# Second projection of 16 expert tiles: fp32 matmuls against three fp32r products of high and low halves

## The reference

```python
def hier_moe(u, wg, bg, we, be, w_gate, w_up, w_down):
    ...  # top-1 group, top-2 experts in it, weights in `combine`
    h = jax.nn.silu(jnp.einsum('bld,edf->blef', u, w_gate)) * jnp.einsum('bld,edf->blef', u, w_up)
    return jnp.einsum('blef,ble,efd->bld', h, combine, w_down)
```

## Time and profile before

| | |
|---|---|
| median of 3 runs | 643.33 us (642.3 to 643.43) |
| the profiled execution | 642.99 us |
| its span, first to last instruction | 641.1 us |
| PE busy | 606.9 us, 95% |
| DVE busy | 441.7 us, 69% |
| ACT busy | 304.5 us, 47% |
| POOL busy | 197.2 us, 31% |
| mean granted TensorE clock | 0.989 |

### The profile page before, as it was taken

The page is one execution under the profiler, slowest core; times in us unless marked ns, Lnnn a source line. Parts: engine busy times, 40 slices in busy tenths (PEclk is TensorE's granted clock), DMA queues, the critical chain, the costliest instruction groups (busy, mean ns, idle before and its releaser), DMA issues.

```text
span 641.1 us, 9310 instructions
## 1 busy us (share of the span) xinstructions
PE 606.9 (95%) x3342; PEld 455.6 (71%) x3342; DVE 441.7 (69%) x754; ACT 304.5 (47%) x503; POOL 197.2 (31%) x159
## 2 busy tenths in 40 slices
PE   6899999999999989998999999989999999999794
PEld 2237899999999966567888888656676776765241
DVE  4957776834993664466662698979998887761197
ACT  2749122334435534006895333926656665753144
POOL 1002333345561307141593071321211212211431
PEclk9999999999999999999999999999999999999798
DMA  8886856574721279855870824968999999999687
GB/s 302 356 274 252 281 183 188 184 236 150 231 80 65 91 255 335 320 210 165 274 238 8 291 73 164 321 243 335 357 389 412 393 384 395 374 352 388 219 263 131
DMA packets 47872, 162.88 MB, mean 254 GB/s; under 512 B 7073, under 2 KB 24865, under 8 KB 35282
## 3 DMA queue, kind: packets, MB, share of 16 engines
q1 hardware_dynamic: 34392, 118.03, 52.0%
q0 software_dynamic: 7712, 20.65, 10.4%
q10 hardware_dynamic: 5722, 23.60, 9.6%
HBM read 140.79 MB, written 31.36 MB: 269 GB/s over the span
## 4 chain that ended last, share of the span: by engine, by line
PE 82%; DVE 7%; DMA 6%; ACT 2%; issue 2%; ACTq 0%; DVEq 0%; POOLq 0%; POOL 0%
PE bank L1886 14%; PE bank L1566 12%; PE bank L1567 12%; PE bank L1940 9%; PE bank L1762 9%; DMA arena<-in_w_mod 3%; PE bank L1402 3%; PE bank L1873 3%; PE bank L1739 3%; PE bank L1666 2%; PE bank L1469 2%; PE bank L2005 2%; PE bank L1722 2%; PE bank L1997 1%; PE bank L1617 1%
## 5 line engine op out<-in xcount | busy, mean ns | idle before, releaser
L746 POOL TENSOR_TENSOR w_low<-arena,w_high 128x1024 fp32r<-128x1024 f32 x22 | 54.1, 2463 | 147.5 <-ACT w_high L954 147.5
L2533 DVE TENSOR_TENSOR gate_up_low<-arena,gate_up_high 128x1024 fp32r<-128x1024 f32 x64 | 75.3, 1221 | 13.1 <-ACT gate_up_high L1238 11.4
L1238 ACT ACTIVATE gate_up_high<-arena 128x1024 fp32r<-128x1024 f32 x64 | 63.9, 1054 | 15.4 <-DMA arena<-in_moe_w_gu 15.4
L954 ACT ACTIVATE w_high<-arena 128x1024 fp32r<-128x1024 f32 x22 | 23.2, 1059 | 87.4 <-PE bank L1567 85.4
L1566 PE MATMUL bank<-u_high,w_high 128*128 128x320 f32 x176 | 56.3, 320 | 1.7 <-DVE u_low L2146 1.7
L1940 PE MATMUL bank<-arena 128*128 128x512 f32 x128 | 57.7, 593 | 0.0
L1567 PE MATMUL bank<-u_high,w_low 128*128 128x320 f32 x176 | 54.4, 309 | 0.0
L1566 PE MATMUL bank<-u_low,w_high 128*128 128x320 f32 x176 | 54.4, 309 | 0.0
L1566 PE MATMUL bank<-u_high,w_low 128*128 128x320 f32 x176 | 54.4, 309 | 0.0
L1567 PE MATMUL bank<-u_low,w_high 128*128 128x320 f32 x176 | 54.4, 309 | 0.0
L1567 PE MATMUL bank<-u_high,w_high 128*128 128x320 f32 x176 | 54.4, 309 | 0.0
(11 more groups left out here) (440 smaller groups left out, 1405.8 us busy)
## 6 DMA issues: line engine op xcount, KB each, us to landing
arena<-in_moe_w_gu SPq DMA_DIRECT2D x38, 1024.0 KB, 11.9
arena<-in_w_mod SPq DMA_DIRECT2D x24, 1024.0 KB, 7.1
y_scr<-arena SPq DMA_DIRECT2D x26, 512.0 KB, 8.5
arena<-in_moe_w_down ACTq DMA_DIRECT2D x13, 1024.0 KB, 9.8
arena<-in_w_in SPq DMA_DIRECT2D x11, 1024.0 KB, 6.5
arena<-in_moe_w_down SPq DMA_DIRECT2D x6, 1024.0 KB, 10.4
arena<-in_x SPq DMA_DIRECT2D x10, 512.0 KB, 7.7
arena<-in_rpb SPq DMA_DIRECT2D x32, 128.0 KB, 3.2
```

Of the source, the lines that this page charges most:

```text
L746: G.tensor_tensor(WL[s_][:, :, w], ring[s_][:, :, w], WH[m % 2].bitcast(F), ALU.subtract).then_inc(wl_rdy, 1)
L954: S.activation(WH[m % 2], ring[(m // 2) % 2][:, :, (m % 2) * P:(m % 2 + 1) * P], ACT.Copy).then_inc(wh_rdy, 1)
L1238: S.activation(WGH[j][c], raw_gu[s][:, c, :, :], ACT.Copy).then_inc(wgh_rdy, 1)
L2533: tt_(WGL[s][c], raw_gu[s][:, c, :, :], WGH[j][c].bitcast(F), ALU.subtract).then_inc(wgl_rdy, 1)
```

## The change

The second projection of the static tiles is made of three fp32r products. ScalarE writes the high half of the transposed hidden rows (`hidden_high`) and, in a buffer of its own for each of the two row blocks k, the high half of the down weights (`down_high`, two instructions behind `hidden_high`). VectorE writes the low half of the hidden rows (`hidden_low`, behind the routing work, in front of pieces 2 and 3), and now increments `ht_ev`. GpSimd writes the low half of the down weights in place (`down_low`, two instructions, called in iteration n for tile n-2, behind the gather of n and the scatter of n-4). TensorE's `down` issues 12 matmuls in place of 4. In GpSimd's queue the scatter of tile 15 goes behind the overflow gather. The overflow step's own second projection stays fp32.

```diff
+        WDL = [split_view(f"down_low{s}", RAW_DN[s], 2, D) for s in range(3)]
+        WDH_AT = [MTAT + 4096, AFTER1 + 12288]
+        WDH = [split_view(f"down_high{k}", WDH_AT[k], 1, D)[:, 0, :] for k in range(2)]
+        HTH = [split_view(f"hidden_high{j}", HTAT + 512 * j, 2, P) for j in range(2)]
+        HTL = [split_view(f"hidden_low{j}", HTAT + 512 * j + 256, 2, P) for j in range(2)]
...
# GpSimd
+            def down_low(n):
+                for k in range(2):
+                    eng.wait_ge(wh_rdy, 30 + 2 * n + k + 1)
+                    G.tensor_tensor(WDL[n % 3][:, k, :], raw_dn[n % 3][:, k, :], WDH[k].bitcast(F), ALU.subtract).then_inc(wl_rdy, 1)
...
                 if n >= 4:
                     rows_scattered(n - 4)
-            for n in range(NE - 3, NE):
-                rows_scattered(n)
+                if n >= 2:
+                    down_low(n - 2)
+            rows_scattered(NE - 3)
+            down_low(NE - 1)
+            rows_scattered(NE - 2)
             eng.wait_ge(slots_rdy, 3)
...
                 token_rows(1, tokens_ov[:, :])
+            rows_scattered(NE - 1)
...
# ScalarE
-            def hidden_copy(n, j):
-                since(eng, ht_mm, n + 1)
-                since(eng, dn_mm, n - 1)
-                S.activation(hT[j][:, :, :], B[6][:, 0:2 * P].rearrange("p (a b) -> p a b", a=2), ACT.Copy
-                             ).then_inc(ht_ev, 1)
+            def hidden_high(n, j):
+                eng.wait_ge(ht_mm, n + 1)
+                since(eng, dn_mm, n - 1)
+                S.activation(HTH[j], B[6][:, 0:2 * P].rearrange("p (a b) -> p a b", a=2), ACT.Copy).then_inc(uth_rdy, 1)
+            def down_high(n):
+                eng.wait_ge(wdn_in[n % 3], 16 * (n // 3 + 1))
+                since(eng, dn_mm, n)
+                for k in range(2):
+                    S.activation(WDH[k], raw_dn[n % 3][:, k, :], ACT.Copy).then_inc(wh_rdy, 1)
...
-                hidden_copy(n, j)
+                hidden_high(n, j)
+                down_high(n)
...
# TensorE, down(n, j, s)
-                since(eng, ht_ev, n + 1)
-                since(eng, wdn_in[s], 16 * (n // 3 + 1))
+                eng.wait_ge(ht_ev, n + 1)
                 since(eng, y_evA, n)
                 since(eng, y_evB, n)
-                for b in range(2):
-                    for k in range(2):
-                        last = mm(B[4 + b][:, :], hT[j][:, k, :], raw_dn[s][:, k, b * 512:(b + 1) * 512],
-                                  start=(k == 0), stop=(k == 1))
+                halves = [slice(512 * b, 512 * (b + 1)) for b in range(2)]
+                for k in range(2):
+                    eng.wait_ge(wh_rdy, 30 + 2 * n + k + 1)
+                    for q, h in enumerate((HTH, HTL)):
+                        for b in range(2):
+                            mm(B[4 + b][:, :], h[j][:, k, :], WDH[k][:, halves[b]], start=(k == 0 and q == 0), stop=False)
+                for k in range(2):
+                    eng.wait_ge(wl_rdy, 30 + 2 * n + k + 1)
+                    for b in range(2):
+                        last = mm(B[4 + b][:, :], HTH[j][:, k, :], WDL[s][:, k, halves[b]], start=False, stop=(k == 1))
                 last.then_inc(dn_mm, 1)
...
# VectorE
+            def hidden_low(n, j):
+                eng.wait_ge(uth_rdy, KT + TT + n + 1)
+                since(eng, dn_mm, n - 1)
+                tt_(HTL[j], B[6][:, 0:2 * P].rearrange("p (a b) -> p a b", a=2), HTH[j].bitcast(F), ALU.subtract).then_inc(ht_ev, 1)
...
                 elif 6 <= n < 6 + TT:
                     last_rows(n - 6)
+                hidden_low(n, j)
                 if n + 2 < NE:
```

More of the change, by code:

```diff
@@ L118, in build @@
         XTL = [split_view(f"xt_low{j}", AFTER1 + 15360 + j * 1024, KT, P) for j in range(2)]
+        WDL = [split_view(f"down_low{s}", RAW_DN[s], 2, D) for s in range(3)]
+        WDH_AT = [MTAT + 4096, AFTER1 + 12288]
+        WDH = [split_view(f"down_high{k}", WDH_AT[k], 1, D)[:, 0, :] for k in range(2)]
+        HTAT = AFTER1 + 17408 + 1024
+        HTH = [split_view(f"hidden_high{j}", HTAT + 512 * j, 2, P) for j in range(2)]
+        HTL = [split_view(f"hidden_low{j}", HTAT + 512 * j + 256, 2, P) for j in range(2)]
         WOH_AT = [SM, SM + 2048, SM + 4096, LATE0 + 28672]
@@ L321, in build @@
         hh = [small.take(2, FE) for _ in range(2)]
-        hT = [small.take(2, P) for _ in range(2)]
+        assert small.at == HTAT
+        hT = small.take(2, P)
+        small.take(3 * 2 * P)
         assert small.at <= late.end
         DG = Region(RAW_GU[0], 2 * TT * P).take(TT, 2, P)
-        last_ = Region(AFTER1 + 12288, 1024)
+        last_ = Region(WO0 - 1088, 1088 - 120)
         LR = last_.take(TT, P)
@@ L1295, in silu_tanh, with unit_hidden @@
                 S.activation(hh[j][:, 0, :], B[j][:, 0:FE], ACT.Tanh, scale=0.5).then_inc(th_rdy, 1)
-            def hidden_copy(n, j):
-                since(eng, ht_mm, n + 1)
+            def hidden_high(n, j):
+                eng.wait_ge(ht_mm, n + 1)
                 since(eng, dn_mm, n - 1)
-                S.activation(hT[j][:, :, :], B[6][:, 0:2 * P].rearrange("p (a b) -> p a b", a=2), ACT.Copy
-                             ).then_inc(ht_ev, 1)
+                S.activation(HTH[j], B[6][:, 0:2 * P].rearrange("p (a b) -> p a b", a=2), ACT.Copy).then_inc(uth_rdy, 1)
[4 more added lines that the diff above has]
+                    S.activation(WDH[k], raw_dn[n % 3][:, k, :], ACT.Copy).then_inc(wh_rdy, 1)
+            def unit_hidden(n):
+                eng.wait_ge(ht_mm, eng.snap(n + 1))
+                eng.wait_ge(dn_mm, NE)
+                S.activation(hT, B[6][:, 0:2 * P].rearrange("p (a b) -> p a b", a=2), ACT.Copy).then_inc(ht_ev, 1)
             def rows_out(n, j):
@@ L1380, in _ @@
                 unit_rows(n + 1)
-                hidden_copy(n, 0)
+                unit_hidden(n)
                 rows_out(n, 0)
@@ L1914, in unit_down @@
                             lanes = slice(UNIT * g, UNIT * (g + 1))
-                            last = mm(B[4 + b][lanes, :], hT[0][:, k, lanes], unit_dn[g][:, k, b * 512:(b + 1) * 512],
+                            last = mm(B[4 + b][lanes, :], hT[:, k, lanes], unit_dn[g][:, k, b * 512:(b + 1) * 512],
                                       start=(k == 0), stop=(k == 1))
```

## The result

Changed kernel: 675.65 us median of 4 runs (674.34 to 677.39); before, on the same chip: 642.82 (639.98 to 643.43). Ratio **1.051, 95% interval 1.048 to 1.054: slower**. The forecast of 686 had the sign and the mechanism, and the time lies in its range of 658 to 700; it was 10 us too long. The profiled execution took 677.39, its span is 675.5.

A forecast was written before the change was run, and what follows sets the result against it. TensorE bounds the kernel now; VectorE, blocked by GpSimd's subtractions, would bound the changed tiles. 643.0 + 41.4 for the tiles (TensorE's 10.7 saving lies inside) + 2.0 for the tail gives 686 us, range 658 to 700.

The forecast's parts named there:

- Bound: Expert tiles: TensorE sets the time before, VectorE and DMA engines just under it; after the change VectorE is the bound.
- 2.73 per second projection: TensorE in each tile: twelve fp32r matmuls take 2.73 us in place of 3.44, saving 0.71 per tile.
- no charge: ScalarE: two more weight copies, 2.0 us per tile, taking it to 8.3 of 10, cost nothing; in the tail nothing waits.
- 2.36 per subtraction: GpSimd in each tile: two subtractions of 128x1024 at 2.36 us each, 4.72 us together.
- Exclusion: Expert tiles: VectorE instructions with all inputs from SBUF and GpSimd's subtractions block each other whole; without it about 634.
- 4.12 us lost per tile: VectorE in tile 1: GpSimd's first subtraction costs it 2.36 us, the second, partly covered, 1.76.
- Tail, +2: After tile 14: later low halves and a gather begun 1.4 us later; charged 2 us, between 0.5 and 4.
- 2 to 3 to spare: Tail: the last store begins some 5 us later, and row gathers waiting for it keep 2 to 3 us spare.
- 1: Expert tiles: no exclusion in this stage, TensorE stays the bound, so faster, 634; chance 0.05.
- 2: Expert tiles: no exclusion, but gathers come late behind the low halves in GpSimd's queue; 642 to 653, chance 0.05.
- 3: TensorE's clock: idling 2 to 4 us per tile could halve it; 700 to 765 if that lasts, chance 0.09.
- 4, better packing: Expert tiles: VectorE and GpSimd interleave better than charged, between lower bound and forecast; 656 to 675, chance 0.15.

The follow-up runs named there:

- e1: Changed kernel, but GpSimd subtracts only 8 of each half's 1024 columns and TensorE's last four products read the high half of the weights; 644.71 us, ratio 1.003.
- e2: Changed kernel, but GpSimd writes zeros in place of each subtraction and TensorE's last four products read the high half of the weights; 657.49 us, ratio 1.022.
- e12: The kernel with zero writes in place of GpSimd's subtractions, but GpSimd copies the weights onto themselves, one read and one write; 672.78 us, ratio 1.047.
- e5: Kernel before the change, with only the scatter of tile 15 issued behind the overflow gathers; 644.98 us, ratio 1.001.
- e6: Changed kernel with only the order undone, the scatter of tile 15 ahead of the overflow gathers again; 677.08 us, ratio 1.052.
- e8: Changed kernel with the scatters of tiles 12 and 13 moved ahead of down_low(13) and down_low(14) on GpSimd's queue; 677.43 us, ratio 1.052.

## Why the prediction was right, and where it was off

- *Bound.* Right that VectorE takes over from TensorE. It had put the DMA engines just under it in the later tiles; the trace of e1 points to them as the bound there once VectorE is not.
- *TensorE*, 2.73 per second projection: right, the one of tile 14 ran without a wait from 615.87 to 618.60.
- *ScalarE*, no charge: right in the tiles, e1 has its copies and cannot be told from the kernel before. "Nothing waits" on it in the tail was wrong, as the point on the tail says.
- *VectorE*, `hidden_low` 0.44: measured 0.42.
- *GpSimd*, 2.36 per subtraction: 2.35 to 2.40 undisturbed.
- *Exclusion.* Shown by e1, e2 and e12, which differ in how much GpSimd reads. It is wider on one side than the prediction had it, as `TENSOR_SCALAR` is held back by writes too, and narrower on another: beside GpSimd's subtractions a `TENSOR_REDUCE` of 128x160 kept its 0.32 (at 454.63) and a `TENSOR_SCALAR` of 128x1 its 0.13 (at 507.93), each seen once. Of the 32 instructions at L2401 about ten lay beside subtractions; it is half only if GpSimd's additions of the same shape count. Of the 35.5 us lost in tiles 0 to 14, 28.7 lie between the changed kernel and e2 (175.45 to 146.75), 5.7 between e2 and e1, 1.1 between e1 and before. The rule of the Trainium skill ("SBUF — State Buffer", "Who interferes with whom") that a GpSimd instruction which only writes SBUF does not block VectorE's two inputs agrees with e2's 1.22.
- *The step that was mis-sized: 4.12 us lost per tile, "takes the next slot whole: 2.36" and then 1.76.* Measured 3.7 in tile 10: 2.2 and 1.5; in tiles 1 to 9 it was 3.3 to 3.8, in tile 0 4.1 for 4.72, in tiles 11 to 13 3.5 for 3.7. The prediction charged GpSimd's whole 2.36 for the first wait, though its own row of 113.93 has 2.16 lost (2.32 for 0.16). Which instruction is hit was not always `gate_up_low` either: in tiles 0, 1 and 6 both waits fell on the routing work. The rest is VectorE's own work, 8.5 us in tile 10 for the 8.7 charged. Tile 0 took 14.5 for 14.6, tiles 1 to 5 67.0 for 70.3, 6 to 10 61.2 for 64.0, 11 to 13 32.8 for 33.8. These are the 7.2 us between 614.9 and 607.66.
- *Tail, +2.* The span behind gating of tile 14 is 67.8 us, where the forecast comes to 69.6 (684.5 less 614.9). In the prediction's terms, from the last product of tile 14 on, the tail grew by 0.9 (618.8 to 675.5, 585.3 to 641.1 before) for the 2 charged. The size was near, the mechanism another one. The chain ran over the scatter of tile 12, issued behind `down_low(13)`, which held ScalarE's copy of tile 14 until 620.1, some 1.4 us after TensorE's last product of that tile (four at 617.68, 1.08 long). The clock gave time back: the 24 matmuls of the overflow step took 3.63 for 5.48. Of the "2 to 3 to spare" for the row gathers nothing was left: TensorE's matmuls did not wait for them, its weight loads did, once, for 0.5 us. In e5, the order alone, the chain runs over the passed store.
- *Rivals.* 1 fell. 2 exists: the late gathers have a part in the 5.7 us that the tiles of e2 take over e1, where 8 had been worked out, and they are hidden in the changed kernel, whose tiles are longer than it asks for. 3: up to the last matmuls of the tail the granted clock was 0.50 in three short stretches only, 3 to 7 us each, one of them behind 3.29 us in which TensorE stood still:

```profile
444.57 1.22 PE L1973 MATMUL bank<-down_high,hidden_high 128*128 128x512 f32 x2 [3.29 <-DVE hidden_low L2724]
```

```profile
443.50:450.20 6.70, 5.63 (x15) 4.36 (x15) 6.56 (x12) 0.90 (x2) 0.00 (x0) 0.50 0.69 289
```

VectorE set that tile's length anyway. The one that cost something lies in the tail: the 48 matmuls at 628.08 took 8.66 us, 7.07 before. The kernel before has a stretch of 6.6 us from 600 us on, which the changed one has not. 4, better packing (656 to 675), is where the time nearly came out; most of that is the mis-sized term.

## What to carry to other kernels

Work moved to an idle GpSimd is not free if it reads SBUF: count VectorE's SBUF-fed instructions beside it, not GpSimd's busy share. Where VectorE can do the same subtraction in half of GpSimd's time, try it on VectorE even when VectorE is the bound; here that was 16 us shorter, though still slower than the kernel before. Work on GpSimd that only writes spares VectorE's two-input subtractions but not its `TENSOR_SCALAR`; VectorE work fed from PSUM kept its time beside either. And before shortening TensorE's work, see that the DMA share of the stage is not already near 1.

## What was not expected of the hardware

- Writes of GpSimd hold back VectorE's `TENSOR_SCALAR` (0.84 for 0.34 on average in e2) and leave its two-input subtractions alone (1.22).
- GpSimd stretches as well, which the prediction had: a 1.04 us copy took 1.92 and a 2.36 us subtraction up to 3.37 where VectorE had begun first. What it had not was the sum: GpSimd's busy time in the page (89.6 us for 32 subtractions) is 14 us more than its work.
- A scatter of 512 KB took 8.9 (e5) and 11.1 us (changed kernel) to land beside the weight loads; passing it is no gain where what comes next reads it back.

Left open: the sizes of the order's and the scatters' effects in the changed kernel (e6, e8), which lie inside the intervals, how e2's and e12's times divide, whether the weights' bytes are the bound once VectorE is not, and whether VectorE's order could put more PSUM-fed work beside the subtractions; that was not tried.
